# Gate and up bias of experts 2 to 31: copied into PSUM by ScalarE instead of added by products

## The chip, the cores and the metric

The kernel runs on one core of one Trainium2 chip. The metric is device time in microseconds (us), the median of several executions. Instructions run on TensorE (PE), VectorE (DVE), ScalarE (ACT) and GpSimd (POOL), each of which works through its own list in order; SyncE (SP) issues the weight loads. They wait for one another through semaphores.

## What is computed

An encoder block on 512 tokens of width 1024: a layer norm, two mixers (gated linear attention and forgetting attention), a second norm, then a mixture of 32 experts, of which each token takes 4, and a last norm. The change concerns the experts only:

```python
gu = xb @ w_gate_up[e] + b_gate_up[e]
gate = jnp.minimum(gu[:, :D_FF], SWIGLU_LIMIT)
up = jnp.clip(gu[:, D_FF:], -SWIGLU_LIMIT, SWIGLU_LIMIT)
glu = gate * jax.nn.sigmoid(SWIGLU_ALPHA * gate)
return ((up + 1.0) * glu) @ w_down[e] + b_down[e]
```

Everything is float32; `xb` holds up to 128 tokens of one expert, `w_gate_up[e]` is 1024x2048, `w_down[e]` 1024x1024.

## The kernel before, in words

**Precision.** A float32 product is made of three: weights and activations are each split into a high part (rounded by a cast on ScalarE, `whi`) and a remainder (a subtraction on VectorE, `wlo`, L1456), and `passes` (L1705 to L1711) adds high x high, high x remainder and remainder x high into PSUM.

**Tiles.** One expert is 12 weight tiles of 1 MB: eight for gate and up (`GUC`), each 128 rows of the 2048 columns, and four for down (`DNC`). SP loads them in order into six buffers; each tile passes through `step_hi` on ScalarE (L997 by way of `tile_hi`), `step_lo` on VectorE, then twelve products of 512 columns on TensorE. Four buffers hold the split tiles, so the high part of tile n waits until TensorE has used tile n-4 (`tile_used`).

**The order of the passes.** Each engine has a function `body(i)`, written out by hand, that is run for i = 1 and 2 and then in a loop for 3 to 30; expert 0 stands in front and expert 31 behind. `body(i)` on TensorE: the eight gate and up tiles of expert i into `psA` (four banks, 2048 columns); `gate_up_bias(i)` (L2120): in each bank a product of two rows of ones with the bias's high and remainder rows (`bgu`), then `gu_done`; the transposes of the next expert's tokens (`turn_x`, L1716); the four down tiles of expert i-1; the transposes of the activation of expert i (`turn_a`, L1716), which wait for `act_ready`. The next body's first product waits for `up_ev`, the second clip.

`body(i)` on ScalarE: the high parts of tiles 4 to 11 of the pass, the high part of the turned tokens (L1049), SiLU (`silu`, L1053), the high parts of tiles 0 to 3 of the next pass, the copy of y out of PSUM (`y_evac`, L1064), the high part of the turned activation.

`body(i)` on VectorE: remainders of tiles 4 to 8, the indices of the next gather, remainders of tiles 9 to 11, `swiglu_in(i)` (waits for `gu_done`; the two clips, L1532 and L1534, which read `psA`), the remainder of the tokens (L1525), the remainder of tile 0 of the next pass, `swiglu_out(i)` (waits for SiLU; the product `act_t`, L1540, then `act_ready`), remainders of tiles 1 to 3, the remainder of the turned activation. These lines, cut to the core:

```python
            swiglu_in(i)
            turned_lo(xT_hi_s, i + 2, xT_hi, xT_lo, xT_lo_s)
            step_lo(i + 1, 0)
            swiglu_out(i)
            for c in range(1, XSPL):
                step_lo(i + 1, c)
```

`body(i)` on GpSimd: two loads of 8 KB with the next bias (`load_bgu`, L676, after `gu_done`), the gather of tokens for a later expert (`gather`, L660), the scatter of the finished rows of y onto the output in DRAM (`scatter`, L671, waits for `y_ready` and the scatter before). The bias had been split on the chip at the start and lies in DRAM (`bgu_dram`).

## Time and profile before

| | |
|---|---|
| three runs | 1759.18, 1759.49, 1761.78 us |
| median | 1759.49 us |
| span of the profiled execution, first to last instruction | 1757.9 us |
| median above that span | 1.6 us |
| share of the chain that ended last: TensorE, VectorE, ScalarE | 87%, 5%, 3% |

The profile shows one execution by its span. No device time of that execution on its own is given, so the 1.6 us between its span and the median of the runs stands for what lies around it. The granted clock of TensorE was 0.996 of 2.4 GHz on average. A row of the timeline gives the start, the time taken (of several merged instructions, from the first to the last), engine, line, operation, output and inputs, and in brackets the idle time before it and what ended it. A matmul's recorded time overlaps the next one's, so that its start and the next start tell the pace.

### The profile page before, as it was taken

What the parts mean: (1) busy time and instruction counts of PE and PEld (TensorE: products, weight loads), DVE (VectorE), ACT (ScalarE), POOL (GpSimd) and SP (SyncE); (2) the same over time, 40 slices, a digit from 0 to 9 for tenths busy, and PEclk for the clock granted to TensorE, in tenths of its full rate; (3) what the DMA queues carried; (4) which work ended last, traced back from release to release, by engine and by line L of the source; (5) the groups of instructions that cost most, each with busy time, mean ns of one, the idle gap of its engine ahead of it and who ended that gap; (6) DMA issues with size and microseconds to landing.
All of it is one profiled execution on the core that took longest, in us unless ns stands there. A gap on an engine that the chain in (4) does not pass through costs nothing.

```text
span 1757.9 us, 23535 instructions
## 1 busy us (share of the span) xinstructions
PE 1732.5 (99%) x8315; PEld 1412.0 (80%) x8316; DVE 1339.2 (76%) x1169; ACT 1119.8 (64%) x957; POOL 286.9 (16%) x227
## 2 busy tenths in 40 slices
PE   9999999999999999999999999999999999999996
PEld 7777888888887777888778888888888888888885
DVE  6323324343346899998999999999999999999998
ACT  5534334473222467777777777777777777777777
POOL 3000000000001262221212122212221212121211
PEclk9999999999999999999999999999999999999998
DMA  8322231212332699999999999999999999999995
GB/s 290 96 96 72 74 94 51 70 56 88 104 136 85 209 362 391 354 379 379 379 381 378 364 381 378 373 366 387 373 377 369 389 370 370 378 386 370 370 369 208
DMA packets 115696, 487.96 MB, mean 278 GB/s; under 512 B 18915, under 2 KB 49635, under 8 KB 66496
## 3 DMA queue, kind: packets, MB, share of 16 engines
q1 hardware_dynamic: 99576, 455.76, 67.4%
q0 software_dynamic: 16064, 31.54, 6.4%
q8 instruction: 32, 0.52, 0.1%
q14 instruction: 16, 0.13, 0.0%
q10 hardware_dynamic: 8, 0.01, 0.0%
HBM read 476.22 MB, written 28.36 MB: 287 GB/s over the span
## 4 chain that ended last, share of the span: by engine, by line
PE 87%; DVE 5%; ACT 3%; issue 3%; DMA 2%; POOLq 0%; DVEq 0%; ACTq 0%; POOL 0%; SPq 0%
PE psA L1709 21%; PE psA L1711 20%; PE psA L1710 20%; PE psX L1711 5%; PE psX L1710 5%; PE psX L1709 5%; PE psX L1716 3%; DVE wlo L1456 3%; DMA raw<-in_w_down 2%; ACT whi L997 1%; PE psX L1903 1%; PE psX L1888 1%; PE psA L2120 1%; PE psX L1912 1%; PE psA L2000 0%
## 5 line engine op out<-in xcount | busy, mean ns | idle before, releaser
L1456 DVE TENSOR_TENSOR wlo<-raw,whi 128x2048 fp32r<-128x2048 f32 x382 | 863.2, 2288 | 64.3 <-ACT whi L997 63.1
L997 ACT CAST whi<-raw 128x2048 fp32r<-128x2048 f32 x382 | 724.5, 1913 | 200.2 <-PE psA L1711 166.7
L1709 PE MATMUL psA<-whi,xT_hi 128*128 128x512 f32 x1036 | 408.8, 395 | 1.9 <-issue 1.9
L1711 PE MATMUL psA<-whi,xT_lo 128*128 128x512 f32 x1036 | 404.4, 390 | 0.0
L1710 PE MATMUL psA<-wlo,xT_hi 128*128 128x512 f32 x1036 | 404.2, 390 | 0.0
L1709 PEld LDWEIGHTS psA<-whi,xT_hi 128*128 128x128 f32 x1036 | 195.1, 188 | 43.1 <-issue 3.9
L1711 PEld LDWEIGHTS psA<-whi,xT_lo 128*128 128x128 f32 x1036 | 194.9, 188 | 40.7
L1710 PEld LDWEIGHTS psA<-wlo,xT_hi 128*128 128x128 f32 x1036 | 195.2, 188 | 39.6 <-issue 0.5
L1709 PE MATMUL psX<-whi,aT_hi 128*128 128x512 f32 x496 | 196.0, 395 | 0.0
L1711 PE MATMUL psX<-whi,aT_lo 128*128 128x512 f32 x496 | 193.6, 390 | 0.0
L1710 PE MATMUL psX<-wlo,aT_hi 128*128 128x512 f32 x496 | 193.5, 390 | 0.0
L1177 DVE TENSOR_TENSOR wlo<-raw,whi 128x2048 fp32r<-128x2048 f32 x40 | 92.4, 2311 | 121.4 <-ACT whi L774 121.4
L1709 PE MATMUL psA<-hT_hi,whi 128*128 128x512 f32 x416 | 164.6, 396 | 0.0
L1711 PE MATMUL psA<-hT_hi,wlo 128*128 128x512 f32 x416 | 162.2, 390 | 0.0
L671 POOL DMA_INDIRECT acc_dram<-y_t,didx x31 | 101.2, 3263 | 348.6 <-ACT y_t L1064 276.9
L1710 PE MATMUL psA<-hT_lo,whi 128*128 128x512 f32 x352 | 137.2, 390 | 0.0
L676 POOL DMA_DIRECT2D bgu<-bgu_dram x64 | 38.9, 609 | 482.3 <-PE psA L2120 478.9
L774 ACT CAST whi<-raw 128x2048 fp32r<-128x2048 f32 x40 | 76.5, 1912 | 60.2 <-PE psA L1711 58.6
L1711 PEld LDWEIGHTS psX<-whi,aT_lo 128*128 128x128 f32 x496 | 93.1, 188 | 19.5
L1709 PEld LDWEIGHTS psX<-whi,aT_hi 128*128 128x128 f32 x496 | 93.3, 188 | 18.6 <-issue 0.2
L1710 PEld LDWEIGHTS psX<-wlo,aT_hi 128*128 128x128 f32 x496 | 93.3, 188 | 18.4
L1709 PEld LDWEIGHTS psA<-hT_hi,whi 128*128 128x128 f32 x416 | 78.2, 188 | 17.2 <-issue 1.8
(408 smaller groups left out, 2024.7 us busy)
## 6 DMA issues: line engine op xcount, KB each, us to landing
raw<-in_w_gate_up SPq DMA_DIRECT2D x254, 1024.0 KB, 8.6
raw<-in_w_down SPq DMA_DIRECT2D x128, 1024.0 KB, 8.0
raw<-in_w_in SPq DMA_DIRECT2D x32, 1024.0 KB, 5.5
raw<-in_w_gla_proj SPq DMA_DIRECT2D x4, 1024.0 KB, 5.1
raw<-in_w_fox_proj SPq DMA_DIRECT2D x4, 1024.0 KB, 5.1
raw<-in_w_out SPq DMA_DIRECT2D x4, 1024.0 KB, 5.0
xt<-in_x SPq DMA_DIRECT2D x4, 512.0 KB, 7.2
h_dram<-xt POOLq DMA_DIRECT2D x4, 512.0 KB, 6.1
```

Source lines behind the costliest of these rows:

```text
L671: g.indirect_dma_start(acc_dram, bass.IndirectOffsetOnAxis(ap=didx[:, 0:1], axis=0), y_t[:], None, bounds_check=token_bound, oob_is_err=Fa ...
L676: g.dma_start(bgu[part:P:32, :], bgu_rows[part, e, :].rearrange("(n c) -> n c", c=512)).then_inc(bgu_in, 16)
L774: s_.copy(whi[:, c % SPL, :], raw[:, c % RAW, :]).then_inc(hi_ready, 1)
L997: s_.copy(xsplit(c)[0], xraw(slot)).then_inc(hi_ready, 1)
L1177: v.tensor_tensor(wlo[:, c % SPL, :], raw[:, c % RAW, :], whi[:, c % SPL, :].bitcast(F32), ALU.subtract).then_inc(lo_ready, 1)
L1456: v.tensor_tensor(lo, xraw(slot), hi.bitcast(F32), ALU.subtract).then_inc(lo_ready, 1)
L1709: mm(dst, sh, mh, start=first, stop=False)
L1710: mm(dst, sh, ml, start=False, stop=False)
L1711: return mm(dst, sl, mh, start=False, stop=last)
L1716: ins = nc.tensor.transpose(dst[:, k // 4, (k % 4) * P:(k % 4 + 1) * P], src[:, k * P:(k + 1) * P], ident[:])
L1888: ins = mm(psX[:, 2 + b, 0:P], fv[:, h, u, :], probsT[:, b, u * P:(u + 1) * P], start=u == 0, stop=u == t)
L1903: mm(psX[:, b, 0:n], qk[:, 0, h % 2, t * P:(t + 1) * P], qk[:, 1, h % 2, 0:n], start=True, stop=False)
```

## The change

For experts 2 to 31 (index from 0) there are no bias products. GpSimd loads the bias of an expert, 2048 float32 values, as four rows of 512 on partitions 0, 32, 64 and 96 (`load_row`), and spreads each to all 128 partitions with `partition_broadcast` (`spread_row`) into `bias_all`, after the gather and the scatter before have landed. ScalarE copies `bias_all` (128x2048) into `psA` (`seed`), between `silu(i)` and the high part of tile 0 of the next pass, after both clips. All gate and up products of these experts add onto what lies there. TensorE waits for `seeded` instead of `up_ev`; the clips wait for the eighth tile (`tile_used`). Experts 0 and 1 and an overflow loop, which is entered only when an expert has more than 128 tokens, keep the bias products. `lnffn_g` gets another place in SBUF, since `bias_all` lies on its old one. Six semaphores that were used once each are merged into two (one for three products of the first stages, one for three of the overflow list), with the same producers and waiters (not shown in the diff below), which makes room for the new ones.

```diff
@@ -203,7 +203,7 @@
     ridx = at("ridx", 191.78125, [P, TT], U32)
     match = at("match", 104, [P, P])
     tokens = at("tokens", 104.5, [P, P])
-    lnffn_g = at("lnffn_g", 120, [P, D])
+    lnffn_g = at("lnffn_g", 203, [P, D])
     lnffn_b = at("lnffn_b", 172, [P, D])
     raw2 = at("raw2", 128, [P, XRAW - RAW, CE])
     whi2 = at("whi2", 96, [P, CE], F32R)
@@ -224,6 +224,8 @@
     y_t = at("y_t", 176, [P, D])
     bgu = at("bgu", 180, [P, 512], F32R)
     aT_lo = at("aT_lo", 184, [P, KT, P], F32R)
+    bias_row = at("bias_row", 182, [P, 512])
+    bias_all = at("bias_all", 120, [P, 4, 512])
 
     acc = at("acc", 80, [P, TT, D])
 
@@ -411,6 +414,10 @@
         if not isinstance(i, int):
             return STEPC * i + 2 * GUC + DNC
         return STEPC * i + 2 * GUC + DNC if i < E - 1 else NMAIN
+
+    def gu_used(i):
+
+        return STEPC * i + DNC
 
     def xraw(slot):
         return raw[:, slot, :] if slot < RAW else raw2[:, slot - RAW, :]
@@ -676,6 +683,24 @@
                 g.dma_start(bgu[part:P:32, :], bgu_rows[part, e, :].rearrange("(n c) -> n c", c=512)).then_inc(bgu_in, 16)
 
 
+        def load_row(e):
+
+            pool.wait_ge(bias_spread, 4 * (e - 2))
+            g.dma_start(bias_row[0:P:32, :], a["b_gate_up"][0][e].rearrange("(n c) -> n c", c=512)).then_inc(brow_in, 16)
+
+        def spread_row(e):
+
+            pool.wait_ge(brow_in, 16 * (e - 1))
+            pool.wait_ge(xg_in, 16 * e)
+            if isinstance(e, int) and e == 2:
+                pool.wait_ge(gu_done, 2)
+            else:
+                pool.wait_ge(y_out, 16 * (e - 2))
+                pool.wait_ge(seeded, e - 2)
+            pool.sem_inc(spreads, 1)
+            for n in range(4):
+                g.partition_broadcast(bias_all[:, n, :], bias_row[32 * n:32 * n + 1, :]).then_inc(bias_spread, 1)
+
         load_bgu(0)
         gather(None, None)
         for r in range(TT):
@@ -693,7 +718,8 @@
         pool.wait_ge(list_out, 16 * TT * TOPK)
         g.dma_start(ltab[:], list_dram.rearrange("(p e) c -> p e c", p=P)).then_inc(ltab_in, 16)
         pool.wait_ge(routed, 1)
-        pool.wait_ge(gu_done, 2)
+        g.dma_start(bias_row[0:P:32, :], a["b_gate_up"][0][2].rearrange("(n c) -> n c", c=512)).then_inc(brow_in, 16)
+        spread_row(2)
         g.dma_start(lnffn_g[:], bcast(a["ln_ffn_g"][0])).then_inc(lnffn_in, 16)
         g.dma_start(lnffn_b[:], bcast(a["ln_ffn_b"][0])).then_inc(lnffn_in, 16)
 
@@ -708,9 +734,10 @@
 
         def body(i, last):
             if not last:
-                pool.wait_ge(gu_done, i + 1)
-                load_bgu(i + 1)
+                if not isinstance(i, int) or i >= 2:
+                    spread_row(i + 1)
                 if not isinstance(i, int) or i < E - 2:
+                    load_row(i + 2)
                     gather(i + 3, i + 2)
             if isinstance(i, int) and 3 <= i < 3 + TT:
                 add_bias(i - 3, i)
@@ -1052,6 +1079,11 @@
             act.wait_ge(gate_min, i + 1)
             s_.activation(act_t[:], gate_t[:], ACT.Silu, scale=SLOPE).then_inc(silu_done, 1)
 
+        def seed(e):
+            act.wait_ge(up_ev, e)
+            act.wait_ge(bias_spread, 4 * (e - 1))
+            s_.copy(psA[:], bias_all[:]).then_inc(seeded, 1)
+
         def y_evac_over(j, free):
             act.wait_ge(tile_used, NMAIN + STEPC * j + STEPC)
             act.wait_ge(tab_ready, free)
@@ -1084,6 +1116,7 @@
             step_hi(1, c)
         turned_hi(xt_done, 3, xT_hi, xT_hi_s)
         silu(1)
+        seed(2)
         for c in range(XSPL):
             step_hi(2, c)
         y_evac(0, 4)
@@ -1106,6 +1139,7 @@
                     stage(1)
             turned_hi(xt_done, i + 2, xT_hi, xT_hi_s)
             silu(i)
+            seed(i + 1)
             for c in range(XSPL):
                 step_hi(i + 1, c)
             y_evac(i - 1, i + 3)
@@ -1528,7 +1562,17 @@
             return tile.rearrange("t (q k p) -> t q k p", p=P, k=2)
 
         def swiglu_in(i):
-            dve.wait_ge(gu_done, i + 1)
+            if isinstance(i, int) and i < 2:
+                dve.wait_ge(gu_done, i + 1)
+            else:
+                dve.wait_ge(tile_used, gu_used(i))
+            clip(i)
+
+        def swiglu_in_over(j):
+            dve.wait_ge(gu_done, 3 + j)
+            clip(E + j)
+
+        def clip(i):
             v.tensor_scalar(by_pair(gate_t), psA[:, 0:2, :].rearrange("t b (q p k) -> t (b q) k p", p=P, k=2), LIMIT,
                             None, ALU.min).then_inc(gate_min, 1)
             v.tensor_scalar(by_pair(up_t), psA[:, 2:4, :].rearrange("t b (q p k) -> t (b q) k p", p=P, k=2), LIMIT,
...
@@ -2069,22 +2113,34 @@
...
         def tile_ready(n):
             pe.wait_ge(hi_ready, NCD + n + 1)
             pe.wait_ge(lo_ready, NCD + n + 1)
+
+        def gate_up_seeded(n, c):
+
+            tile_ready(n)
+            hi, lo = xsplit(c)
+            for b in range(4):
+                cols = slice(b * 512, (b + 1) * 512)
+                mm(psA[:, b, :], xT_hi[:, c, :], hi[:, cols], start=False, stop=False, skip_group_check=True)
+                mm(psA[:, b, :], xT_hi[:, c, :], lo[:, cols], start=False, stop=False, skip_group_check=True)
+                ins = mm(psA[:, b, :], xT_lo[:, c, :], hi[:, cols], start=False, stop=c == KT - 1,
+                         skip_group_check=True)
+            ins.then_inc(tile_used, 1)
 
         def gate_up(n, c, parts, after_first=False):
 
@@ -2176,9 +2232,12 @@
             if first:
                 pe.wait_ge(gate_min, 1)
             else:
-                pe.wait_ge(up_ev, i)
+                pe.wait_ge(seeded, i - 1)
             for c in range(GUC):
-                gate_up(tile_no(i, c), c, (xT1_hi, xT1_lo) if first else (xT_hi, xT_lo), first and c == 0)
+                if first:
+                    gate_up(tile_no(i, c), c, (xT1_hi, xT1_lo), c == 0)
+                else:
+                    gate_up_seeded(tile_no(i, c), c)
                 if first:
                     if c == 2:
                         turn_a(0, 1)
@@ -2200,7 +2259,8 @@
                 if second and c == 5:
                     pe.wait_ge(stage_ready, TT)
                     gate_bias(1)
-            gate_up_bias(i)
+            if first:
+                gate_up_bias(i)
             if second:
                 pe.wait_ge(stage_ready, 2 * TT)
             split_ready(aT_hi_s, aT_lo_s, i)
@@ -2220,14 +2280,13 @@
             body(i)
 
         split_ready(xT_hi_s, xT_lo_s, E)
-        pe.wait_ge(up_ev, E - 1)
+        pe.wait_ge(seeded, E - 2)
         for c in range(GUC):
-            gate_up(tile_no(E - 1, c), c, (xT_hi, xT_lo))
+            gate_up_seeded(tile_no(E - 1, c), c)
             if c == 2:
                 split_ready(aT_hi_s, aT_lo_s, E - 1)
                 pe.wait_ge(match_seq, 1)
                 mm(psT[:, 0, 0:P], ones[:], tokens[:], start=True, stop=True).then_inc(match_seq, 1)
-        gate_up_bias(E - 1)
         pe.wait_ge(y_ready, E - 2)
         for q in range(DNC):
             if q == DNC - 1:
```

## Rows read from the trace of the kernel before

**Rows 1.** The page: the span, and each engine's busy time.
```profile
span 1757.9 us, 23535 instructions
...
PE 1732.5 (99%) x8315; PEld 1412.0 (80%) x8316; DVE 1339.2 (76%) x1169; ACT 1119.8 (64%) x957; POOL 286.9 (16%) x227
```

**Rows 2.** Busy time by stretch: one pass (busy; clock, DMA share, GB/s last).
```profile
1240.04:1275.06 35.02, 35.02 (x165) 28.81 (x165) 32.91 (x21) 26.43 (x17) 7.49 (x4) 1.00 0.96 376
```

**Rows 3.** Chain of waits, same pass: start, us, what.
```profile
1261.81 0.44 PE psA L2120 x2
1262.25 1.02 PE psX L1716 x8
...
1274.19 0.87 PE psX L1716 x8
1275.06 0.23 PE psA L1709
```

**Rows 4.** Timeline of VectorE, same pass: start, us, instruction, [idle before].
```profile
1261.08 2.29 DVE L1456 TENSOR_TENSOR wlo<-raw,whi 128x2048 fp32r<-128x2048 f32 x1 [0.43 <-ACT whi L997]
1263.79 2.29 DVE L1456 TENSOR_TENSOR wlo<-raw,whi 128x2048 fp32r<-128x2048 f32 x1 [0.42 <-ACT whi L997]
1266.00 1.22 DVE L1532 TENSOR_SCALAR gate_t<-psA 128x1024 f32<-128x1024 f32 x1
1267.13 1.21 DVE L1534 TENSOR_SCALAR up_t<-psA 128x1024 f32<-128x1024 f32 x1
...
1270.14 2.29 DVE L1456 TENSOR_TENSOR wlo<-raw,whi 128x2048 fp32r<-128x2048 f32 x1 [0.66 <-ACT whi L997]
1272.35 1.22 DVE L1540 SCALAR_TENSOR_TENSOR act_t<-up_t,act_t 128x1024 f32<-128x1024 f32 x1
```

**Rows 5.** Timeline of ScalarE, same pass.
```profile
1261.85 1.91 ACT L997 CAST whi<-raw 128x2048 fp32r<-128x2048 f32 x1 [0.80 <-PE psA L1711]
...
1267.25 1.06 ACT L1053 ACTIVATE act_t<-gate_t 128x1024 f32<-128x1024 f32 x1 [2.58 <-DVE gate_t L1532]
1268.22 5.51 ACT L997 CAST whi<-raw 128x2048 fp32r<-128x2048 f32 x3
```

**Rows 6.** Timeline of GpSimd, same pass: the scatter.
```profile
1243.02 3.66 POOL L671 DMA_INDIRECT acc_dram<-y_t,didx  x1 [11.01 <-ACT y_t L1064]
```

**Rows 7.** DMA issues, 1200 to 1300 us: count, KB, median us to landing.
```profile
bgu<-bgu_dram POOLq DMA_DIRECT2D x6, 8.0 KB, 5.2
acc_dram<-y_t,didx POOLq DMA_INDIRECT x3, 12.2
```

**Rows 8.** Timelines of GpSimd and VectorE near 40 us: they meet.
```profile
39.53 1.09 POOL L614 TENSOR_SCALAR_AFFINE_SELECT sel<-sel 32x1024 fp32r<-32x1024 f32 x1
39.66 3.11 DVE L1177 TENSOR_TENSOR wlo<-raw,whi 128x2048 fp32r<-128x2048 f32 x1 [4.33 <-ACT whi L774]
...
40.69 3.03 POOL L614 TENSOR_SCALAR_AFFINE_SELECT sel<-sel 32x1024 fp32r<-32x1024 f32 x1
```

**Rows 9.** Timeline of GpSimd, expert 1: the list table's load.
```profile
664.59 0.60 POOL L694 DMA_DIRECT2D ltab<-list_dram  x1 [5.63 <-DMA list_dram<-lval,lidx]
```

**Rows 10.** Timeline of ScalarE, expert 1: SiLU.
```profile
666.96 1.06 ACT L1053 ACTIVATE act_t<-gate_t 128x1024 f32<-128x1024 f32 x1 [3.25 <-DVE gate_t L1532]
```

**Rows 11.** Chain of waits, expert 1: turn_a.
```profile
673.34 1.09 PE psX L1716 x8
```

**Rows 12.** Timeline of TensorE: two resumptions after idle time.
```profile
607.11 0.47 PE L2110 MATMUL psA<-whi,xT_hi 128*128 128x512 f32 x1 [0.85 <-ACT xT_hi L1069]
...
634.39 0.47 PE L1709 MATMUL psA<-whi,xT_hi 128*128 128x512 f32 x1 [1.90 <-issue]
```

**Rows 13.** Busy time by stretch: the granted clock is third from the end.
```profile
606.00:612.00 6.00, 5.14 (x23) 3.96 (x23) 5.16 (x4) 2.49 (x2) 4.61 (x8) 1.00 0.58 150
...
635.50:636.00 0.50, 0.50 (x3) 0.40 (x2) 0.50 (x1) 0.38 (x1) 0.00 (x0) 0.50 1.21 115
...
638.50:639.00 0.50, 0.50 (x2) 0.40 (x2) 0.50 (x2) 0.01 (x1) 0.25 (x1) 0.59 1.09 459
```

More of the change, by code:

```diff
@@ L310, in build @@
     act_half, dve_half = S("act_half"), S("dve_half")
-    small_done, smT_evac = S("small_done"), S("smT_evac")
-    fl_done, fl_evac = S("fl_done"), S("fl_evac")
-    gate_pre, la_ln, la_ready = S("gate_pre"), S("la_ln"), S("la_ready")
+    smT_evac = S("smT_evac")
+    fl_evac = S("fl_evac")
+    low_product, la_ln, la_ready = S("low_product"), S("la_ln"), S("la_ready")
     suf_done, kd_exp, kd_mul = S("suf_done"), S("kd_exp"), S("kd_mul")
@@ L351, in build @@
     bgu_in = S("bgu_in")
+    brow_in, bias_spread, seeded = S("brow_in"), S("bias_spread"), S("seeded")
+    spreads = S("spreads")
     acc_in = [S(f"acc_in{t}") for t in range(TT)]
@@ L887, in hook @@
             if s == 3:
-                act.wait_ge(small_done, 1)
+                act.wait_ge(low_product, 1)
                 for r in range(TT):
@@ L893, in hook @@
             if s == 4:
-                act.wait_ge(fl_done, 1)
+                act.wait_ge(low_product, 2)
                 s_.copy(fl[:], psX[:, :, 0:FH]).then_inc(fl_evac, 1)
             if s == 5:
-                act.wait_ge(gate_pre, 1)
+                act.wait_ge(low_product, 3)
                 log_sigmoid_tail(la[:], psX[:]).then_inc(la_ln, 1)
@@ L1689, in _ @@
                     tile_lo(c % XRAW, NMAIN + STEPC * j + c, c)
-                swiglu_in(E + j)
+                swiglu_in_over(j)
                 swiglu_out(E + j)
@@ L1806, in hook @@
                                  (hT_hi[:, k, :], hT_lo[:, k, :]), k == 0, k == KT - 1)
-                ins.then_inc(small_done, 1)
+                ins.then_inc(low_product, 1)
             if s == 4:
@@ L1813, in hook @@
                              start=True, stop=True)
-                ins.then_inc(fl_done, 1)
+                ins.then_inc(low_product, 1)
             if s == 5:
@@ L2071, in overflow_counts @@
                 ins = mm(psX[0:3 * E, 1, 0:1], member3[:, t, :], ones[:, 0:1], start=t == 0, stop=t == TT - 1)
-            ins.then_inc(counts_done, 1)
+            ins.then_inc(ov_product, 1)
         def overflow_ranks():
             pe.wait_ge(flag_ready, 2)
-            mm(psX[0:3 * E, 1, 1:2], strict[0:3 * E, 0:3 * E], ovflag[:], start=True, stop=True).then_inc(pre_done, 1)
+            mm(psX[0:3 * E, 1, 1:2], strict[0:3 * E, 0:3 * E], ovflag[:], start=True, stop=True).then_inc(ov_product, 1)
         def overflow_list():
@@ L2261, in _ @@
                     gate_up(NMAIN + STEPC * j + c, c, (xT_hi, xT_lo))
-                gate_up_bias(E + j)
+                gate_up_bias(2 + j)
                 turn_a(E + j, E + j)
```

17 lines of the change are left out of this document (8 added, 9 removed).

## Prediction, made before the changed kernel was run

> **What bounds the kernel now.** I read the page first: TensorE is busy for 99% of a span of 1757.9 us [rows 1]. Then one pass of the expert loop in the table by stretch: 35.02 us, all of it TensorE, VectorE busy 32.91, ScalarE 26.43, GpSimd 7.49, at full granted clock [rows 2]. Thirty experts run at that pace, so whatever shortens TensorE's list shortens the time, if the other engines keep up. The chain of waits gives the order inside a pass [rows 3]: the last gate and up product ends at 1261.81, the bias products take 0.44, the eight transposes of the next tokens 1.02, the four down tiles run until 1274.19, the eight transposes of the activation (turn_a) take 0.87, and at 1275.06 the next expert starts. Call 1261.81 T; T is the moment on which the others hang.
>
> Then the two engines that prepare turn_a, from the timelines. ScalarE starts the last weight split of the pass at T+0.04, idles 2.58 us, runs SiLU at 1267.25, and goes straight on to the next expert's splits at 1268.22 [rows 5]. VectorE does the last remainder at 1263.79, the two clips at 1266.00 and 1267.13, a remainder of the tokens, then, in the order written in its body, first the next expert's remainder 0 at 1270.14 (it had waited 0.66 for ScalarE's split 0) and only then the product act_t at 1272.35 [rows 4]. That ends at 1272.35+1.22 = 1273.57. TensorE wants it at 1274.19: **the slack is 0.62 us**, and it is the number on which this change turns. ScalarE's 26.43 of 35.02 looks like room, but it is room elsewhere in the pass.
>
> **The change, part by part.** *Removed:* the bias products, 0.44 us of TensorE a pass [rows 3]. There are 30 of them (experts 2 to 31); the last lies where the chain is no longer TensorE's, so 29 count. Also removed are two 8 KB loads a pass from POOL's queue; nobody waits for them in a pass, so nothing.
>
> *Added on ScalarE:* a copy of 128x2048 from SBUF into PSUM, between SiLU and the next expert's split 0. No row has that direction. The nearest is the split, 128x2048 from SBUF to SBUF, 1.91 us [rows 5]; I take 1.91 and keep 1.6 to 2.1 as bounds (estimates: a sixth less, a tenth more). It waits for the second clip (1267.13+1.21 = 1268.34), so it starts where split 0 did, and split 0 moves from 1268.22 to about 1270.2, by 1.98. Behind it on VectorE: remainder 0 moves from 1270.14 to 1272.12, act_t from 1272.35 to 1274.33, its end from 1273.57 to 1275.55. TensorE, with 0.44 less in front, would now ask at 1273.75. It stands idle for 1.8 us, and turn_a starts at about 1275.6 instead of 1274.19: **+1.4 us a pass**, with the saving already in it. TensorE's next product needs the seed only after turn_a, so that wait costs nothing. The later splits 1 to 3, the copies of y and of the turned activation have TensorE's eight tiles (21.8 us) in front of their next use and catch up: ScalarE had 0.80 us idle before each split and VectorE 0.43 before each remainder [rows 4, 5].
>
> *Moved on VectorE:* the clips wait for the last tile instead of the bias products. They were not waiting for those: they start at 1266.00, when VectorE comes free, 4.2 us after T. Nothing. The wait for tokens that TensorE transposes 0.44 earlier gains nothing for the same reason.
>
> *Added on GpSimd:* four broadcasts of 512 columns a pass and one load. They may start when the previous scatter has landed: issued at 1243.02 [rows 6], 12.2 us to land [rows 7], so 1255.2, and the seed wants the last at 1268.4: a window of 13.2 us. Behind them on POOL stand the row load, the gather and the scatter; the gather's tokens are used one pass later, so its cover is some 20 us. No row shows a broadcast. Nearest is a GpSimd operation that reads and writes SBUF, 1024 columns on 32 partitions in 1.09 us undisturbed; half of it, 0.55, is my lower bound. Upper bound: the 3.03 us that such an operation took when it was disturbed [rows 8]. I take b = 1.1, as a broadcast also has to cross partitions.
>
> The same rows show what disturbs: one such operation began at 39.53, VectorE's remainder at 39.66 took 3.11 us instead of 2.29 and the next GpSimd operation, recorded at 40.69, 3.03 instead of 1.09 [rows 8]. They take turns. So in the window each broadcast waits for a remainder to end, and the next remainder waits for the broadcast, beyond its 0.43 of idle time. Laid into the pass: two broadcasts hold VectorE back by b-0.43 each, 1.3 us, of which the following gaps give some back; the other two fall beside the clips, which read PSUM, and end about 2b = 2.2 us behind the first clip's start, just before the seed could start anyway. Net I take **+0.5 a pass** (0 if they never meet; 0.2 to 0.9 for b up to 1.2; beyond that the seed waits for the last broadcast and each 0.1 us of b costs four times that).
>
> By the Trainium skill, "SBUF — State Buffer", in its account of the shared port pair, a VectorE instruction with two SBUF inputs and a GpSimd instruction that reads SBUF exclude one another for the whole instruction; the two rows agree with that (3.11 and 3.03 us), and without the rule the term would be 0.
>
> *The clock.* TensorE had idled 1.90 us before 634.39 [rows 12]; about a microsecond after it resumed the granted clock was at 0.50, and it rose again in the stretch that ends at 639 [rows 13]. That is some 3.4 us at the lower level (1.2 GHz), 1.7 us lost. The 0.85 us of idle before 607.11 [rows 12] left it at 1.00 [rows 13]. The new idle time, 1.8 plus 0.5, lies above both. I count a fall in six passes of ten: **+1.0 a pass**; bounds 0 and 1.7.
>
> *The first seeded expert.* Its row is requested behind the load of the list table, at 664.59+0.60 = 665.2 [rows 9]. A load of 8 KB takes 5.2 us to land [rows 7]: 670.4. Four broadcasts, 4.4: 674.8. Seed 1.9, split 1.9, remainder 2.2, act_t 1.2: turn_a at 682.1, where it was at 673.34 [rows 11]; SiLU had been done at 668.0 [rows 10]. That is 8.8 once (6.6 at b = 0.55, 16.4 at b = 3), and 1.7 for the clock: **+10.5**. By the Trainium skill, "GPSIMD Engine Reference", Instruction dispatch, the first call of freshly loaded code costs about 6 us more; no row here shows it, and the sum with it would be 1860.
>
> **Sum.** 29 passes of 1.4+0.5+1.0 = 2.9 are 84.1, with 10.5 it is 94.6 against the span of 1757.9: 1852.5. The median of the runs lies 1.6 above that span, so **1854**. The semaphores that are merged and the moved gain row cost nothing: each wait has the same producer as before.
>
> **Rivals.** *The clock holds* (the new idle time too short, or broken by the transposes): 29 x 1.9 + 8.8 = 63.9, so 1823. For it: only one fall is recorded. If it falls in every pass: 29 x 3.6 + 10.5, 1874.
> *GpSimd becomes the bound.* At b = 2 the broadcasts, in turn with remainders, end some 3.2 us behind the seed's moment, beyond the 0.9 already counted: a pass of about 40.5 to 42, 1757.9+1.6+29 x 6.5+14 = 1962. At b = 3, near 2080. For it: its indirect transfers take 3.66 us [rows 6]; against it: these read an index and write descriptors, and the plain operation took 1.09.
> *It ends faster.* Place: turn_a. If split 0 is late by less than 0.62-0.44 = 0.18 us, TensorE never waits, and 29 x 0.44 = 12.8 are won: 1746.7. Between 0.18 and 0.62 it is a draw. Against it: a whole copy of 2048 columns stands in front of split 0, ten times the 0.18, and remainder 0 follows split 0 by 0.02 us. It could only be so if the copy into PSUM took almost nothing.
>
> **How the numbers follow.** Forecast (clock falls in some or all passes, broadcasts short): 0.55, own range 1835 to 1885. Clock holds: 0.28. GpSimd bound: 0.12. Faster or equal: 0.05. The range must hold 8 in 10: from 1802 (no meeting of the two engines and no clock loss give 29 x 1.4 + 6.6, so 1807; a quicker copy takes off the rest) up to 1925 (b near 1.6, or a clock lost each pass with b = 1.4). A difference of 0.2% (3.5 us) is what this kernel's measurement can tell from none. Faster 0.03, same 0.02, slower 0.95.
>
> **What would show it.** Right: 30 copies into psA of near 1.9 us on ScalarE; turn_a's transposes waiting for act_t in each pass, some 2 us (29 waits, 50 to 70 in total); a pass of 37 to 38.5; VectorE's remainders longer than 2.29 where a broadcast runs; granted clock below 1.00 in the loop; a first wait of some 9 us near 673. Wrong: a pass of 34.6 (the faster rival); ScalarE's copy waiting for a broadcast in each pass (GpSimd bound); waits for act_t with the clock at 1.00 throughout (clock holds); remainders all at 2.29 (no meeting).

## The result, and the profile after

The changed kernel takes **1852.12 us** (median of 4 runs, 1851.01 to 1853.16) against 1759.34 of the kernel before: ratio 1.0526, 95% interval 1.0514 to 1.0539. The forecast was 1854. The page, the slices left out, then the shares of its chain of waits:

```profile
span 1850.0 us, 23489 instructions
PE 1746.4 (94%) x8195; PEld 1428.0 (77%) x8196; DVE 1344.0 (73%) x1169; ACT 1176.5 (64%) x987; POOL 476.6 (26%) x317
...
PE 70%; issue 11%; DVE 9%; ACT 8%; POOL 1%; DMA 1%; ACTq 0%; DVEq 0%; POOLq 0%
```

TensorE fell from 99% to 94% busy [rows 1]. The table by stretch, for two passes that follow one another (from turn_a to turn_a; busy by engine, then granted clock, DMA share, GB/s):

```profile
1297.24:1334.18 36.94, 34.75 (x160) 28.64 (x161) 32.82 (x21) 28.34 (x19) 13.64 (x7) 1.00 0.93 356
...
1334.18:1372.67 38.49, 36.31 (x161) 29.96 (x161) 33.09 (x21) 28.34 (x19) 13.05 (x7) 0.96 0.90 344
```

A pass took 35.02 [rows 2]. Now one without a fall of the clock takes 36.9, one with it 38.4 to 38.5 (the second: its transposes, in the timeline below, take 1.77 us at the lower level instead of 1.09). Of the 29 waits for act_t in front of turn_a of experts 2 to 30, 13 were followed by such a fall, of 3.4 us each; 12 of these lie in the 29 passes up to expert 30's turn_a, the last one behind it. The timelines of the first of the two passes, VectorE, ScalarE, TensorE, GpSimd (start, us, instruction, idle before and what ended it); T, the end of the last gate/up product, is 1320.24:

```profile
1324.42 1.22 DVE L1576 TENSOR_SCALAR gate_t<-psA 128x1024 f32<-128x1024 f32 x1
1325.56 1.22 DVE L1578 TENSOR_SCALAR up_t<-psA 128x1024 f32<-128x1024 f32 x1
1326.69 1.22 DVE L1559 TENSOR_TENSOR xT_lo<-psX,xT_hi 128x1024 fp32r<-128x1024 f32 x1
1330.63 2.29 DVE L1490 TENSOR_TENSOR wlo<-raw,whi 128x2048 fp32r<-128x2048 f32 x1 [2.72 <-ACT whi L1024]
1332.84 1.22 DVE L1584 SCALAR_TENSOR_TENSOR act_t<-up_t,act_t 128x1024 f32<-128x1024 f32 x1
```
```profile
1325.67 1.06 ACT L1080 ACTIVATE act_t<-gate_t 128x1024 f32<-128x1024 f32 x1 [2.59 <-DVE gate_t L1576]
1326.88 1.87 ACT L1085 COPY psA<-bias_all 128x2048 f32<-128x2048 f32 x1
1328.69 7.31 ACT L1024 CAST whi<-raw 128x2048 fp32r<-128x2048 f32 x4
```
```profile
1297.24 1.09 PE L1760 MATMUL psX<-ident,act_t 128*128 128x128 f32 x8 [2.19 <-DVE act_t L1584]
...
1334.18 1.77 PE L1760 MATMUL psX<-ident,act_t 128*128 128x128 f32 x8 [2.19 <-DVE act_t L1584]
```
```profile
1312.95 9.49 POOL L702 PARTITION_BROADCAST bias_all<-bias_row  x4 [9.92 <-DMA acc_dram<-y_t,didx]
```

Read against [rows 4, 5]: SiLU still follows the gate clip; the seed copy starts at T+6.64 and lasts 1.87; split 0 starts at T+8.45 where it was at T+6.41; remainder 0 follows it (2.72 us idle `<-ACT whi`, it was 0.66), act_t ends at T+13.82 and turn_a starts 0.12 later, after 2.19 us without work. The broadcasts end at 1322.44, 4.4 us before the seed. The waits (in us: total, times, longest) and the broadcast's line seen by itself (durations in ns, minimum/median/maximum), then the remainder's:

```profile
PE psX L1760 <- DVE act_t L1584: 77.2, 30, 14.1
...
POOL bias_all L702 <- DMA acc_dram<-y_t,didx: 210.5, 23, 10.3
...
ACT psA L1085 <- POOL bias_all L702: 12.0, 1, 12.0
```
```profile
L702 POOL PARTITION_BROADCAST bias_all<-bias_row x120: 793/2822/2896, 681.1 to 1770.1; - x120
L702 POOLq MODIFY_POOL_CONFIG  x2: 5/5/5, 675.6 to 675.6; - x2
...
L1490 DVE TENSOR_TENSOR wlo<-raw,whi x382: 2270/2291/2745, 612.4 to 1825.4; 128x2048 fp32r<-128x2048 f32 x191
```

Thirty waits for act_t, but only one of the seed for a broadcast. That one is the first seeded expert (GpSimd, ScalarE, TensorE):

```profile
668.97 0.62 POOL L721 DMA_DIRECT2D bias_row<-in_b_gate_up  x1
681.08 2.80 POOL L702 PARTITION_BROADCAST bias_all<-bias_row  x4 [11.50 <-issue]
```
```profile
683.97 1.87 ACT L1085 COPY psA<-bias_all 128x2048 f32<-128x2048 f32 x1 [11.99 <-POOL bias_all L702]
```
```profile
691.18 1.97 PE L1760 MATMUL psX<-ident,act_t 128*128 128x128 f32 x8 [14.06 <-DVE act_t L1584]
```

The row landed at 675.1, the pool configuration came at 675.6, and from there nothing is recorded for 5.5 us. And the start of the kernel differs, before and after (GpSimd; the third row is TensorE, after):

```profile
2.08 0.29 POOL L565 TENSOR_SCALAR_AFFINE_SELECT ident<-ident 128x128 f32<-128x128 f32 x1 [0.24 <-POOL ident L564]
```
```profile
12.79 1.38 POOL L572 TENSOR_SCALAR_AFFINE_SELECT ident<-ident 128x128 f32<-128x128 f32 x1 [10.97 <-issue]
...
14.22 1.11 PE L1782 MATMUL psX<-ident,xt 128*128 128x128 f32 x4 [4.44 <-POOL ident L572]
```

**Where the 92.1 us of span lie**, by the starts of turn_a: up to expert 0's, 648.24 against 644.27, +4.0; expert 0's to expert 1's, 42.94 against 29.07, +13.9; the 29 passes from expert 1's to expert 30's, 1093.5 against 1021.0, +72.6; behind it 65.3 against 63.6, +1.7, which is the thirteenth fall (experiments 3 to 7 have none there and take 63.7). The first seeded expert reaches into the first of the 29 passes: TensorE's clock was at the lower level from 679.1 to 696.2, and that pass took 41.65 us, 4.7 above the 36.9.

### The profile page after: what moved, and what is told of

It is laid out like the page before. It is cut to its first block, busy times and chain, and to the rows that moved or that the text cites. A ratio compares the mean times of both kernels' runs of the same rounds, so it can differ in the third digit from the quotient of the medians.

```text
span 1850.0 us, 23489 instructions
## 1 busy us (share of the span) xinstructions
PE 1746.4 (94%) x8195; PEld 1428.0 (77%) x8196; DVE 1344.0 (73%) x1169; ACT 1176.5 (64%) x987; POOL 476.6 (26%) x317
## 4 chain that ended last, share of the span: by engine, by line
PE 70%; issue 11%; DVE 9%; ACT 8%; POOL 1%; DMA 1%; ACTq 0%; DVEq 0%; POOLq 0%
PE psA L2139 12%; PE psA L2140 12%; PE psA L2141 12%; PE psA L1753 9%; PE psA L1754 8%; PE psA L1755 8%; ACT whi L1024 6%; PE psX L1760 2%; DVE gate_t L1576 2%; DVE act_t L1584 2%; DVE up_t L1578 2%; DVE wlo L1490 2%; PE psX L1947 1%; PE psX L1932 1%; POOL list_dram L655 1%
## 5 line engine op out<-in xcount | busy, mean ns | idle before, releaser
L2139 PE MATMUL psA<-whi,xT_hi 128*128 128x512 f32 x960 | 384.0, 400 | 0.0
L2140 PE MATMUL psA<-wlo,xT_hi 128*128 128x512 f32 x960 | 378.9, 395 | 0.0
L2141 PE MATMUL psA<-whi,xT_lo 128*128 128x512 f32 x960 | 378.0, 394 | 0.0
L702 POOL PARTITION_BROADCAST bias_all<-bias_row x120 | 278.8, 2425 | 277.1 <-DMA acc_dram<-y_t,didx 210.5
L2139 PEld LDWEIGHTS psA<-whi,xT_hi 128*128 128x128 f32 x960 | 184.7, 192 | 39.7 <-issue 1.5
L2141 PEld LDWEIGHTS psA<-whi,xT_lo 128*128 128x128 f32 x960 | 183.4, 191 | 39.2
L2140 PEld LDWEIGHTS psA<-wlo,xT_hi 128*128 128x128 f32 x960 | 184.4, 192 | 37.5
L678 POOL DMA_INDIRECT acc_dram<-y_t,didx x31 | 64.2, 2070 | 416.1 <-ACT y_t L1096 369.6
L1760 PE MATMUL psX<-ident,act_t 128*128 128x128 f32 x256 | 45.0, 333 | 77.2 <-DVE act_t L1584 77.2
```

The source lines that it names most:

```text
L702: g.partition_broadcast(bias_all[:, n, :], bias_row[32 * n:32 * n + 1, :]).then_inc(bias_spread, 1)
L1760: ins = nc.tensor.transpose(dst[:, k // 4, (k % 4) * P:(k % 4 + 1) * P], src[:, k * P:(k + 1) * P], ident[:])
L2139: mm(psA[:, b, :], xT_hi[:, c, :], hi[:, cols], start=False, stop=False, skip_group_check=True)
L2140: mm(psA[:, b, :], xT_hi[:, c, :], lo[:, cols], start=False, stop=False, skip_group_check=True)
L2141: ins = mm(psA[:, b, :], xT_lo[:, c, :], hi[:, cols], start=False, stop=c == KT - 1, skip_group_check=True)
```

## The experiments

Twelve kernels ran. Those with an interval were timed in three or five rounds, the others in one execution. Unless said otherwise the edit is made to the changed kernel.

**1. The split ahead of the seed.** Undoes the place of the copy, keeps its work.
```diff
-            seed(i + 1)
-            for c in range(XSPL):
+            step_hi(i + 1, 0)
+            seed(i + 1)
+            for c in range(1, XSPL):
```


> The changed kernel with one move: ScalarE's copy into PSUM stands behind the high part of tile 0 instead of in front of it. Order theory (the copy costs what it delays tile 0, and with it the product act_t and turn_a): split 0 is back at T+6.4, turn_a waits for nothing, a pass takes 34.6 us instead of 36.9 to 38.5 and the granted clock no longer falls in the loop; the first seeded expert still waits some 8 us for its row. Total near 1757 us. GpSimd theory (the broadcasts are what slows the pass): the pass stays above 36 us and the total above 1800.

Measured 1769.53 us, ratio 1.0073 (1.0056 to 1.0089), a pass of 34.83. TensorE's transposes (first row, its line is 1762 here) still start 0.13 behind act_t's end (second row), after 0.14 us without work:
```profile
1320.37 1.09 PE L1762 MATMUL psX<-ident,act_t 128*128 128x128 f32 x8
...
1319.02 1.22 DVE L1586 SCALAR_TENSOR_TENSOR act_t<-up_t,act_t 128x1024 f32<-128x1024 f32 x1
```
So the copy's place is what costs. But only 0.19 of the 0.44 us a pass came out. The slack of 0.62 was read too large. It took turn_a's start, 1274.19, from the chain of waits [rows 3], which counts a step from the end of the one before. In the timeline of the kernel before the transposes overlap that product and start 0.16 earlier:
```profile
1274.03 1.03 PE L1716 MATMUL psX<-ident,act_t 128*128 128x128 f32 x8
```
So act_t, whose end is at 1273.57, was 0.46 early, the shorter list takes some 0.44 of that, and the 0.13 from its end to the first transpose no longer fit. After such a wait the next product starts 0.89 behind the first transpose, where it was 0.79 (1274.82 in the kernel before). That the whole is still above the kernel before lies outside the ordinary passes: +3.8 up to expert 0's turn_a, and +8.4 for the two passes behind expert 1's, where expert 2's first products wait 6.9 us for the late seed.

**2. The product act_t ahead of remainder 0 on VectorE**, the seed left in front.
```diff
-            step_lo(i + 1, 0)
             swiglu_out(i)
+            step_lo(i + 1, 0)
```


> The changed kernel with one move on VectorE: the product act_t stands in front of the remainder of tile 0. Order theory: the copy still delays split 0 by 1.9 us, but act_t no longer stands behind it and ends at T+8.9; tile 0 is complete at T+12.7, just when TensorE wants it at T+12.8. A pass of 34.6 to 34.9 us, clock at full in the loop, total near 1760 (1757 to 1770). If what TensorE waits for is the seed itself or the broadcasts, the pass stays at 36.9 or more, total above 1830.

Measured 1784.26, ratio 1.0151 (1.0134 to 1.0168), a pass of 35.2. The wait for act_t is gone, the next one took its place:
```profile
PE psA L2139 <- DVE wlo L1490: 26.5, 29, 10.1
PEld psA L2139 <- ACT whi L1024: 21.6, 27, 1.8
```
TensorE now waits for the late split 0 and its remainder behind turn_a: remainder 0 ends at T+12.98, where T+12.7 was expected. Some 0.3 us of that come from the broadcasts: two remainders a pass take up to 2.64 us beside them here, so that the first clip starts at T+4.49 instead of T+4.2. Either queue repaired alone isn't enough.

**3. No copy** (its semaphore is still raised, so the products add onto what the tile before left; the up and gate biases of experts 2 to 31 are missing).
```diff
-            s_.copy(psA[:], bias_all[:]).then_inc(seeded, 1)
+            act.sem_inc(seeded, 1)
```


> The changed kernel without ScalarE's copy (all waits and signals stay, the broadcasts too): the bias is left out and the sums of one expert are added onto those of the last. Order theory: pass of 34.6 us, total near 1760. GpSimd theory: pass stays above 36.

1795.47, a pass of 35.35, so the copy's work is 36.9-35.35 = 1.55 a pass. It isn't the 34.6 that was expected, since ScalarE still waits for the second clip before split 0 (T+6.9 instead of T+6.4), and TensorE still for act_t, 0.64 us a pass:
```profile
1335.63 7.35 ACT L1024 CAST whi<-raw 128x2048 fp32r<-128x2048 f32 x4 [0.39 <-DVE up_t L1578]
```
The wait for the clip alone, without the copy, makes the pass longer than the 35.02 of the kernel before. Some 10 us of this one execution's total are not of the ordinary passes: TensorE stood idle for 3.44 us before 866.68 and for 3.40 before 880.00, behind late remainders, and the clock fell both times. What made them late was not followed.

**4. No broadcasts in the loop** (experts 3 to 31 get expert 2's biases; the edit, in `spread_row`).
```diff
+            if not isinstance(e, int) or e > 2:
+                pool.sem_inc(bias_spread, 4)
+                return
```


> The changed kernel without GpSimd's broadcasts for experts 3 to 31 (row loads, waits, signals and ScalarE's copy stay; each of these experts gets expert 2's bias). Order theory: nothing changes, passes of 36.9 us, 38.5 where the clock falls, total 1852 within 8. My forecast's term of 0.5 us a pass for broadcasts that hold VectorE back: total near 1838. VectorE's remainders are expected at 2.29 us in both kernels.

1852.79. The 29 passes take 1092.5 us against 1093.5, with 12 falls of the clock in either: the 116 broadcasts cost 0.03 a pass. That the totals agree as well is chance: expert 0's to expert 1's turn_a took 5.8 us more here, the start 2.0 less, the tail 1.6 less.

**5. The first bias row and a first small broadcast early**, the four broadcasts ahead of the list table's load (shortened; the lines taken out at the old places are left out).
```diff
+        g.partition_broadcast(bias_row[:, 0:8], ones[0:1, 0:8]).then_inc(spreads, 1)
...
         load_bgu(0)
+        g.dma_start(bias_row[0:P:32, :], <row of expert 2>).then_inc(brow_in, 16)
...
+        spread_row(2)
         g.dma_start(ltab[:], ...)
```


> The changed kernel with the first seeded expert's row and broadcasts earlier: the row's load stands some 70 us ahead, one broadcast of 8 columns some 50 us ahead makes GpSimd load the code for it while it has nothing to do, and the four broadcasts stand in front of the list table's load. Theory (the one-off wait is 6.2 us for the row to land, 5.5 us of code loading and 2.8 us of broadcasts, one behind the other): the wait of 14.1 us before the first seeded expert's turn_a shrinks to about 2, total near 1852 - 13 = 1839. Rival (the wait is for something else, such as the list's indirect transfers): less than 3 us come back. The passes of the loop are to stay as they are.

1845.42, 6.7 below the change where 13 were forecast, and only 3.2 of it lie where the edit is, between expert 0's and expert 1's turn_a (39.70 against 42.94): 2.6 lie in the start, which varies (see experiment 12), and the rest in the tail and the passes. The seed's wait fell from 12.0 to 7.7 only: in this execution the list's last transfers, behind which the broadcasts stand, had landed at 675.2, in the changed kernel's at 668.4.
```profile
661.64 7.39 POOL L657 DMA_INDIRECT list_dram<-lval,lidx  x1 [0.30 <-issue]
...
675.25 2.79 POOL L704 PARTITION_BROADCAST bias_all<-bias_row  x4 [4.93 <-DMA list_dram<-lval,lidx]
```
No idle time put down to issue stands in front of the broadcasts now; the transfer's length changes from execution to execution (7.39 us here, 2.29 in the changed kernel's profile).

**6. The idle time filled:** eight products whose results nobody reads, in front of turn_a's wait.
```diff
+            pe.wait_ge(xT_lo_s, x + 1)
+            if not isinstance(i, int) or 2 <= i < E - 1:
+                for _ in range(8):
+                    mm(psT[:, 0, :], xT_hi[:, 0, :], xT_hi[:, 0:4, :], start=True, stop=True)
             pe.wait_ge(act_ready, i + 1)
-            pe.wait_ge(xT_lo_s, x + 1)
```


> The changed kernel with eight idle products of 512 columns in front of turn_a in each pass, into the PSUM banks that turn_a then overwrites: they fill 1.8 of the 2.2 us for which TensorE waits. Clock theory (the granted clock falls in about half of the passes because of that idle time, at 1.55 us each): no fall in the loop, every pass 36.9 us, total near 1852 - 20 = 1832. Rival (the clock falls for another reason, or turn_a comes later because of the products): total at 1850 or above.

1829.21. Every pass behind the first is 36.8 to 36.9, the granted clock is 1.00 from 696 to 1815 us, and the idle time is 0.30:
```profile
1282.67 1.98 PE L2206 MATMUL psX<-xT_hi 128*128 128x512 f32 x8
1284.95 1.09 PE L1760 MATMUL psX<-ident,act_t 128*128 128x128 f32 x8 [0.30 <-DVE act_t L1584]
```
More work made the kernel 23 us faster. The clock's share is 13 x 1.55 = 20 us, as the longer passes had said (18.6 in the 29 passes, 1.6 in the tail); the rest is passes that are some 0.08 us shorter than the change's without a fall, and the spread of what stands in front of them.

**7. Half the copy** (the up half keeps what was there).
```diff
-            s_.copy(psA[:], bias_all[:]).then_inc(seeded, 1)
+            s_.copy(psA[:, 0:2, :], bias_all[:, 0:2, :]).then_inc(seeded, 1)
```


> The changed kernel with a copy of 128x1024 instead of 128x2048 (the up half gets no bias and adds onto the last expert's sums). Order theory: each us of copy in front of split 0 is a us of a pass; the pass is 36.9 - 0.85 = 36.0 us where the clock holds, between 35.35 (no copy) and 36.9. Clock: the idle time is 1.3 us, and falls should be rarer than 13 in 29. Total 1852 - 29 x 0.85 - some 10 for the clock = 1815 to 1828. If the copy's length did not matter, 1852.

1804.65, a pass of 36.04, and no fall of the clock in the loop at 1.34 us of idle time each. The copy takes 1.02 instead of 1.87, the pass 0.86 less: from the half copy to the whole one, copy time goes into the pass one to one. From no copy (35.35) to the half it is 0.69 for 1.02, since without the copy 0.35 pass between the second clip and split 0. The 1804.65 is below the range expected mainly because the clock held everywhere, which is 20 us instead of the 10 that were counted.

**8. One small broadcast in the kernel before**, nothing else of the change.
```diff
+        pool.wait_ge(xg_in, 32)
+        g.partition_broadcast(w_rt[:, 0, 0:8], ones[0:1, 0:8]).then_inc(blank_ready, 1)
+        pool.wait_ge(blank_ready, 9)
```


> The kernel before with a single broadcast of 8 columns on GpSimd, behind the loads of the last norm's rows in expert 1, where GpSimd has nothing urgent. Code theory: GpSimd holds one set of code at a time, and an execution finds the set that the execution before left; with one broadcast in the kernel, the first affine_select of the next execution must load its code again, about 10.7 us of GpSimd, of which TensorE waits 4.4 for the identity, so the whole kernel is slower by about 4 us (ratio 1.0023, 1762.7 against 1758.6). Rival (the 4 us at the start of the changed kernel have to do with something else in it, such as the moved tensors or the changed semaphores): no difference, ratio 1.0000 within 0.001.

1766.11, ratio 1.0037 (1.0024 to 1.0051). It reproduces the late start and adds a gap of its own, which is the larger part. In its profile, 8.9 us longer than that of the kernel before, 1.6 lie up to expert 0's turn_a, 0.9 up to expert 1's, and the two passes behind it take 8.3 more (43.17 and 37.85), of which GpSimd's idle time in front of the broadcast is the likely cause; the ordinary passes stay at 35.02.
```profile
13.38 0.43 POOL L565 TENSOR_SCALAR_AFFINE_SELECT ident<-ident 128x128 f32<-128x128 f32 x1 [11.56 <-issue]
...
687.39 1.17 POOL L700 PARTITION_BROADCAST w_rt<-ones  x1 [9.96 <-issue]
```

**9. The three moves together** (1, 2 and 5).

> The changed kernel with three moves in the order of issue: the split of the next pass's row 0 goes ahead of the seed on ScalarE, the up activation product goes ahead of the remainder 0 on VectorE, and the first bias row with a first small broadcast comes early, so that the broadcast's code is loaded before an expert needs it. Theory that the pass is set by act_t and the start of the transposes: with both moves act_t ends some 8.5 us after the last gate/up product, ahead of what TensorE has left, and remainder 0 ends at about 11.1, ahead of its need at 12.8; the pass is about 34.6 us, against 35.02 before and 34.85 with the first move alone, which saves 12 us in 29 passes. The one-off at the first seeded expert falls from 14 to 2 us or less; the 4 us at the start of the kernel stay. Sum: 1758.9 - 12 + 2 + 4 = 1753, ratio 0.995 to 0.999. Rival, that GpSimd's broadcasts and the seed still hold the products of the first seeded expert, or that remainder 0 comes late again: 35.2 a pass, 1770.

**1753.06, ratio 0.9968 (0.9957 to 0.9980): faster than both kernels, 0.3% below the one before.** A pass, and where act_t and remainder 0 now stand near its end; the third row is a remainder of the same pass beside a broadcast:
```profile
1306.46:1341.01 34.55, 34.55 (x162) 28.61 (x161) 33.46 (x21) 27.95 (x18) 14.13 (x7) 1.00 0.98 381
```
```profile
1337.64 1.21 DVE L1588 SCALAR_TENSOR_TENSOR act_t<-up_t,act_t 128x1024 f32<-128x1024 f32 x1
1338.78 2.28 DVE L1494 TENSOR_TENSOR wlo<-raw,whi 128x2048 fp32r<-128x2048 f32 x1
```
```profile
1328.90 2.75 DVE L1494 TENSOR_TENSOR wlo<-raw,whi 128x2048 fp32r<-128x2048 f32 x1
```
TensorE is busy for all of the pass; turn_a at 1341.01 finds act_t ready for 2.2 us. The 29 passes take 1008.1 us, 12.8 less than before. That this is 29 x 0.44 is in part chance: an ordinary pass gains 0.49 (34.53 against 35.02), as the start of the last gate and up product and that of the first transpose behind it are 0.53 closer without the bias products (0.23 against 0.76), but three passes from 818 us on take 35.9 to 36.2 here, and only two do in the kernel before. The broadcasts now do lengthen VectorE's work: in an ordinary pass the two that follow directly on another remainder take 2.75 instead of 2.29, and the clips start at T+5.0 instead of T+4.2. It costs nothing, since act_t is early enough. Turn_a of expert 1 comes 28.73 after that of expert 0 (29.07 before), so the one-off is gone too. What is left is the start, +5.0, and 1.3 in the tail.

**10. As 9, the identity made by an iota and a comparison on VectorE.**
```diff
-        marks.link(g.memset(ident[:], 0.0))
-        marks.mark(g.affine_select(out=ident[:], in_=ident[:], ...))
+        marks.mark(g.iota(ident[:], [[1, P]], base=0, channel_multiplier=-1, ...))
...
+        v.tensor_scalar(ident[:], ident[:], 0.0, None, ALU.is_equal)
```


> The kernel of the run before it in this list, with the identity matrix for TensorE's first transposes built from a GpSimd iota and a VectorE comparison in place of the memset and the affine select. Theory that the 4 us at the start are GpSimd's wait for the code of the affine select, behind which TensorE's first transposes stand: they go, and the time is 4 us below that of the run before it (about 1749, ratio 0.993 to 0.996 to the kernel before). Rival, that the iota waits for code in the same way, or that the load is only moved to the next custom instruction in front of which TensorE waits: no gain, ratio equal to that of the run before it within 0.001.

1760.30, ratio 1.0002 (0.9994 to 1.0011). The rival's cause held, its number didn't, as the time is 7 us above experiment 9's: the iota waits too, and VectorE's comparison, at 13.39, stands first in VectorE's list, so that the first norm's statistics begin at 13.54 instead of 4.38 and TensorE's first transposes at 18.19. The profiled execution is the fastest of the eleven (1754.64), so where the rest of the median lies isn't seen.
```profile
13.12 0.24 POOL L571 IOTA ident<- 128x128 f32 x1 [11.45 <-issue]
```

**11. As 9, with an affine select of 32 x 8 dead values at the end of GpSimd's list.**

> The kernel with the three moves (the split of the next pass's row 0 ahead of the seed, the activation product ahead of remainder 0, the early bias row with a first small broadcast), and one more GpSimd instruction: an affine select of 32 x 8 values of the bias row, dead by then, behind GpSimd's last queued scatter-add of the tail. Theory that the 11 us in front of the first affine select are the return to the code that this instruction needs, since the execution before ended with the broadcasts' code loaded: now each execution ends with the first code, loaded in the tail where GpSimd waits for VectorE anyway, and the next one starts as the kernel before does, its first affine select 0.3 us behind the memset. The start gives back its 4 to 5 us: about 1748.5 us, ratio 0.993 to 0.995. Rival, that the code is loaded anew in every execution whatever the one before left, or that the load in the tail holds back the last scatter: no gain, ratio 0.9968 or more.

1754.17, ratio 0.9971 (0.9959 to 0.9983): no gain. The affine select at the end ran at once, without a pool configuration in front of it, and the next start waited as ever:
```profile
13.83 0.28 POOL L572 TENSOR_SCALAR_AFFINE_SELECT ident<-ident 128x128 f32<-128x128 f32 x1 [12.01 <-issue]
...
1730.19 1.62 POOL L765 TENSOR_SCALAR_AFFINE_SELECT bias_row<-bias_row 32x8 f32<-32x8 f32 x1
```
So it hadn't loaded anything, and the experiment didn't test what it was meant to. It shows that an affine select can run on what a broadcast leaves, and yet the first affine select of the next execution waits. In each kernel a pool configuration stands in front of the first of these operations (at 2.0 us in the kernel before too); in front of this last one there is none.

**12. As 9, its small broadcast moved to the very start**, ahead of the affine select.
```diff
+        pool.wait_ge(first_fills, 4)
+        g.partition_broadcast(ident[:, 0:8], ones[0:1, 0:8]).then_inc(spreads, 1)
+        pool.wait_ge(spreads, 1)
         marks.link(g.memset(ident[:], 0.0))
```


> The kernel with the three moves, its first small broadcast (8 columns) moved from the expert loop's preparation to the very start, into the identity's columns before they are cleared, so that a broadcast is the first GpSimd operation that needs loaded code. In the run with the affine select at the end no load was recorded with that last affine select (no pool configuration stood in front of it), so it left open whether the 11 us at the start are the return to the first code. Theory that GpSimd holds one set of code, that the first operation chooses it, and that the broadcast's set holds the affine select too: then only one load is in the program, each execution ends with the set that the next one starts with, and the 11 us at the start go: first affine select near 2.5 us, total 1753 - 4.5 = 1748.5, ratio about 0.994. Rival 1, that a second load stands in front of the affine select: start as late as before or later by the broadcast's own load of 6 to 11 us, ratio 1.000 or more. Rival 2, that any program with a broadcast loads its code anew in each execution: 11 us stand in front of the broadcast, no gain, ratio 0.997.

1759.57, ratio 0.9993 (0.9981 to 1.0004). By the total it could be rival 1 (1.000 or more), but the rows decide against both rivals:
```profile
1.82 0.28 POOL L571 PARTITION_BROADCAST ident<-ones  x1
...
2.53 0.29 POOL L575 TENSOR_SCALAR_AFFINE_SELECT ident<-ident 128x128 f32<-128x128 f32 x1 [0.16 <-POOL ident L574]
...
14.63 0.14 POOL L586 IOTA small<- 32x1 f32 x1 [10.55 <-issue]
...
680.16 2.80 POOL L705 PARTITION_BROADCAST bias_all<-bias_row  x4 [13.09 <-issue]
```
The broadcast and the affine select run at once at 1.8 and 2.5: the code that the execution before had used last was still there. A second pool configuration stands in front of the iota, which needs the other set, and its load (10.55 idle) now lies behind the identity. Experiment 11's affine select ran without one, the first of experiment 9 waits behind one: so the set seems to be chosen by what comes first in the program, which no run separates further.

TensorE's first transposes start at 10.52 instead of 14.04 (10.91 in the kernel before), turn_a of expert 0 at 642.37 (644.27 before, and 645.6 to 650.6 in the profiles of the change and of experiments 1 to 9). The spread of the latter goes with the clock between 600 and 645 us: without a fall there it is 645.6 to 646.2 (experiments 4, 5, 8), with 3.4 us at the lower level 648.1 to 648.2 (the change, 1, 6), with 6.8 us 649.3 to 649.7 (3, 9), with 10.2 us 650.4 to 650.6 (2, 7). The kernel before has one such fall, experiment 12 none, so the load at the start itself is worth some 3.3 to 3.8 us.

Lost again in the loop: the iotas had put the broadcasts' set out, it was loaded anew in front of the first seed (13.09 idle, 7.7 of it behind the pool configuration), and expert 2's products waited 12.14 us. A small broadcast at both places should keep the 3 to 8 us, which by estimate would be 1745 to 1750. That kernel wasn't run.

## Why the prediction was right, and which of its terms were not

The total hit by 2 us, with errors of both signs: the 29 passes were forecast at 84.1 and cost 72.6, the rest at 10.5 and cost 19.5. The mechanism was right, but a hit this close is luck: errors of 11.5 and 9.0 us cancel.

- **Slack at turn_a and the copy's place: right.** Split 0 moved by 2.04 (forecast 1.98), the copy took 1.87 (1.91). Experiments 1, 3 and 7 show the chain: copy, split 0, remainder 0, act_t, turn_a. The slack itself was 0.46 and not 0.62 (experiment 1). Idle time 2.19, forecast 1.8 plus 0.5.
- **+1.4 a pass:** a pass without a loss of clock was 36.9, +1.9. Three parts make the difference. 0.16 is the slack's misreading: the forecast 1275.6 was set against 1274.19 instead of 1274.03. 0.17 gathers on the chain from the clips to turn_a, which starts at T+13.96 (median of the passes without a fall) instead of T+13.8. 0.15 is the restart, which I had not counted: from turn_a's start to the next expert's last gate and up product it is 22.96, where it was 22.81.
- **+0.5 for broadcasts that meet remainders: it is 0 in this kernel.** They do meet, four take 9.49 us beside the remainders and 2.80 alone, but nearly all of the wait falls on GpSimd. The remainder's median is 2.291 us, it was 2.289, ten of them take 2.42 to 2.75, in four passes, and experiment 4 gives 0.03 a pass. The step that failed is the size b = 1.1: alone a broadcast takes 0.7. That VectorE yields in its turn was right. Where a remainder follows directly on another and a broadcast stands in between, as in experiment 9, it takes 2.75, 0.46 more; here most have some 0.43 of idle time in front of them, which nearly covers it (an inference from these rows; no run varied that idle time alone). By the Trainium skill, "SBUF — State Buffer", in its account of the shared port pair, the two exclude each other for a whole instruction; the trace agrees, in the broadcasts' times here and in VectorE's in experiment 9. That the 0.5 equals what +1.4 lacked is luck.
- **+1.0 for the clock: right in kind, too large.** 12 falls in the 29 passes (forecast 6 of 10) of 1.55 each (1.7): 0.64 a pass. Experiment 6 shows it. The rival that the clock holds failed for this kernel, though 1.34 us of idle time in experiment 7 left it up.
- **The first seeded expert, +10.5: it cost 13.9.** And that is only up to expert 1's turn_a, where 8.8 had been counted; the clock's part, 1.7 of the 10.5, lies in the pass behind. Two terms were off. The broadcasts took 2.80, not 4.4; and 5.5 us went between the pool configuration and the first one. By the Trainium skill, "GPSIMD Engine Reference", Instruction dispatch, the first call of freshly loaded code costs about 6 us; the trace agrees where a broadcast follows the kernel's other work (5.5 here, 5.7 in experiment 9, but up to 9.7 in experiment 8), and the sum should have had it.
- **The start, +4.0: not foreseen** (+1.4 to +6.3 in the profiles of experiments 1 to 9). The same code load at the other end: experiments 8 and 12 show that a broadcast late in the kernel puts out the set of code that the next execution's first constants want. Some 3.3 to 3.8 us are the load's, the rest of the spread the clock's (experiment 12).
- **GpSimd as the bound: failed.** Its broadcasts end 4.4 us early at 2.4 us each. **Faster:** its condition was that split 0 be late by less than 0.18 us. The condition itself was wrong: in experiment 1 split 0 is at T+6.42, on time, and TensorE still waits and gains only 0.19 a pass. Experiment 9, with split 0 late at T+7.2, gets its 12.8 us in the passes by order: act_t ahead of remainder 0.

## What to carry to other kernels

Where an engine with a third of its time free gets new work, ask what is next in its queue and who waits for that; 0.46 us of slack decided here, not the 26.43 of 35.02. Read such a slack from starts in the timeline; a chain of waits counts overlapping products from the end of the one before. If two engines feed the one that bounds, put what it needs first at the head of both queues: either move alone lost (1.0073, 1.0151), both with the early row won (0.9968). The first move loses outside the ordinary passes; with the early row alone it wasn't run. A GpSimd operation of a new kind is priced with its code: once where it is first used and, in a kernel that begins with operations of another set as this one does, once at the start of every execution.

## What the runs showed of the hardware that was not expected

- GpSimd's code stays from one execution to the next (inferred from repeated executions of one kernel each). The kernel before waits 0.24 us at its first affine select; with a broadcast later in it, 10.9 to 12.3 us pass in front of the first affine select or iota of an execution, and with a broadcast first (experiment 12) 10.6 in front of the first iota. In no kernel did a broadcast follow an iota, or an iota a broadcast, without such a wait; an affine select ran at once behind the broadcast in the same execution (experiments 11 and 12). From the pool configuration to the first broadcast it was 5.5 us in the change, 5.7 in experiment 9, 7.7 in experiment 12, 9.7 in experiment 8. What makes some waits twice as long as others stays open.
- A broadcast of 512 values to 128 partitions takes about 0.7 us alone and a median of 2.82 in the loop, beside VectorE's two-input remainders. It lengthens those from 2.29 to 2.75 where one follows directly on another (two a pass in experiment 9), and seldom where VectorE has idle time in front of them (ten, of up to 2.75, in the change; none above 2.30 in experiment 4, without broadcasts in the loop).
- The clock fell after 13 of 29 idle times of 2.1 to 2.2 us, though the passes are alike, and after none at 1.34 (experiment 7) or 0.64 (experiment 3, whose two falls, at 866.5 and 880.1, stand at idle times of 3.4). What picks the passes stays open.
